# Gate and up projections of three feed-forwards: nine of eleven double turns as seven products of half sums instead of eight

## What is computed

```python
def swiglu(x, w_gu, w_down):
    g, u = jnp.split(x @ w_gu, 2, axis=-1)
    return (jax.nn.silu(g) * u) @ w_down

for l in range(2):
    x = layer_norm(ALPHA * x + 0.5 * swiglu(x, ffn1_w_gu[l], ffn1_w_down[l]), ln1_g[l], ln1_b[l])
    x = layer_norm(ALPHA * x + hybrid_mixer(x, ...), ln2_g[l], ln2_b[l])
    x = layer_norm(ALPHA * x + 0.5 * swiglu(x, ffn2_w_gu[l], ffn2_w_down[l]), ln3_g[l], ln3_b[l])
```

## Time and profile before

| | |
|---|---|
| median of 3 runs | 3521.88 us (3521.74 to 3522.15) |
| span of the profiled execution | 3520.6 us |
| TensorE busy | 3484.5 us (99%), 15956 matmuls |
| VectorE busy | 1960.7 us (56%) |
| ScalarE busy | 1381.0 us (39%) |
| GpSimd busy | 465.3 us (13%) |
| read from memory | 309.25 MB, 89 GB/s over the span |

### The profile page before, as it was taken

How to read it: one execution, slowest core, us unless ns; L and a number is a source line. 1 busy time by engine, 2 the same in 40 slices (tenths; PEclk the granted TensorE clock), 3 DMA queues, 4 the chain that set the end, 5 groups by cost and what they waited for, 6 DMA issues and landing times.

```text
span 3520.6 us, 44495 instructions
## 1 busy us (share of the span) xinstructions
PE 3484.5 (99%) x15956; PEld 2801.7 (80%) x15956; DVE 1960.7 (56%) x2532; ACT 1381.0 (39%) x1951; POOL 465.3 (13%) x321
## 2 busy tenths in 40 slices
PE   9999999999999999999999999999999999999998
PEld 6777888888777788888888876788878887678886
DVE  8888544425888644433543588533263327973324
ACT  5555433323555443323332366423243224662223
POOL 3333010001333110002100211100020003030002
PEclk9999999999999999999999999999999999999999
DMA  3112322223212222222322221222222222122222
GB/s 123 60 66 69 108 94 99 98 96 114 72 61 66 96 96 95 98 99 98 101 95 96 90 72 61 90 95 95 96 90 95 95 96 90 49 78 96 96 98 99
DMA packets 88241, 315.01 MB, mean 89 GB/s; under 512 B 10048, under 2 KB 10560, under 8 KB 87872
## 3 DMA queue, kind: packets, MB, share of 16 engines
q1 hardware_dynamic: 85824, 305.68, 25.9%
q10 hardware_dynamic: 2304, 7.80, 0.6%
HBM read 309.25 MB, written 4.19 MB: 89 GB/s over the span
## 4 chain that ended last, share of the span: by engine, by line
PE 83%; DVE 11%; DVEq 3%; ACT 2%; issue 1%; DMA 0%; SPq 0%; ACTq 0%
PE ps L1847 21%; PE ps L1848 20%; PE ps L1849 20%; PE sc L1847 5%; PE sc L1848 5%; PE sc L1849 5%; DVE w_lo L1121 3%; DVE cc_out L1703 2%; PE ps L2023 1%; DVE h_lo L1601 1%; ACT w_hi L542 1%; PE sc L2095 1%; DVEq L1459 1%; DVEq L1625 1%; PE ps L1946 0%
## 5 line engine op out<-in xcount | busy, mean ns | idle before, releaser
L1121 DVE TENSOR_TENSOR w_lo<-raw,w_hi 128x1024 fp32r<-128x1024 f32 x573 | 739.0, 1290 | 1110.4 <-ACT w_hi L542 1109.9
L542 ACT ACTIVATE w_hi<-raw 128x1024 fp32r<-128x1024 f32 x573 | 606.7, 1059 | 1412.8 <-PE ps L1849 757.2
L1847 PE MATMUL ps<-h_hi,w_hi 128*128 128x512 f32 x2576 | 1043.6, 405 | 9.3 <-DVE w_lo L1121 4.4
L1849 PE MATMUL ps<-h_hi,w_lo 128*128 128x512 f32 x2576 | 1005.4, 390 | 0.0
L1848 PE MATMUL ps<-h_lo,w_hi 128*128 128x512 f32 x2576 | 1004.4, 390 | 0.0
L1847 PEld LDWEIGHTS ps<-h_hi,w_hi 128*128 128x128 f32 x2576 | 484.5, 188 | 139.8 <-issue 40.1
L1849 PEld LDWEIGHTS ps<-h_hi,w_lo 128*128 128x128 f32 x2576 | 483.8, 188 | 103.2
L1848 PEld LDWEIGHTS ps<-h_lo,w_hi 128*128 128x128 f32 x2576 | 485.1, 188 | 92.7 <-issue 4.8
L1847 PE MATMUL ps<-hid_hi,w_hi 128*128 (+1 forms) x792 | 309.7, 391 | 0.0
L1849 PE MATMUL ps<-hid_hi,w_lo 128*128 (+1 forms) x792 | 308.2, 389 | 0.0
L1848 PE MATMUL ps<-hid_lo,w_hi 128*128 (+1 forms) x792 | 308.2, 389 | 0.0
(11 more groups left out here) (312 smaller groups left out, 4327.4 us busy)
## 6 DMA issues: line engine op xcount, KB each, us to landing
raw<-wts SPq DMA_DIRECT2D x573, 512.0 KB, 3.3
x<-xT ACTq DMA_DIRECT2D x1, 2048.0 KB, 7.9
parked<-x ACTq DMA_DIRECT2D x8, 256.0 KB, 2.0
x<-parked ACTq DMA_DIRECT2D x1, 2048.0 KB, 8.1
outT<-x SPq DMA_DIRECT2D x8, 256.0 KB, 2.1
x<-xT SPq DMA_DIRECT2D x5, 256.0 KB, 7.5
x<-xT ACTq DMA_DIRECT2D x3, 256.0 KB, 4.7
raw<-wts SPq DMA_DIRECT2D x2, 256.0 KB, 5.2
```

The source lines that it names most:

```text
L542: act(w_hi[:, s].rearrange("p a b -> p (a b)"), raw[:, s, :], ACT.Copy).then_inc(s_whi, 1)
L1121: tt(w_lo[:, s].rearrange("p a b -> p (a b)"), raw[:, s, :], w_hi[:, s].rearrange("p a b -> p (a b)").bitcast(F32), ALU.subtract).then_inc ...
L1847: mm(out, w_hi[:, s, b, :], hi, start=start, stop=False, skip_group_check=True)
L1849: return mm(out, w_lo[:, s, b, :], hi, start=False, stop=stop, skip_group_check=True)
```

## The change

The last nine double turns of gate/up in f = 3, 4 and 5 are written as a Strassen-Winograd product. The weights of one double turn (two gate tiles and two up tiles) are seen as a 2x2 matrix of blocks: A11 and A12 are the gate weights of the first and second four input tiles, A21 and A22 the up weights. The tokens are quarters: four input tiles by 256 tokens. Where eight products of a block with a quarter give gate and up, seven products of sums do:

| product | weights | tokens | bank |
|---|---|---|---|
| 0 | A11 | first inputs, first tokens | 0 |
| 1 | S2 = A11 + S1 | T2 | 1 |
| 2 | S1 = A21 + A22 | N1 | 2 |
| 3 | S3 = A11 + A21 | N3 | 1, on top |
| 4 | A12 | second inputs, first tokens | 0, on top |
| 5 | A22 | N4 | 1, on top |
| 6 | S4 = A12 + S2 | second inputs, second tokens | 2, on top |

A product is 2 x 4 x 3 = 24 matmuls of 256 columns. The token sums N1, N3, T2, N4 are made once per feed-forward, the weight sums S1 to S4 in every double turn, all by VectorE. All seven weight operands are split on the chip into high and low halves, in three slots (the third lies where `x` was). So `x` is written to memory at the end of the norm before, and read back after the last product. The host lays the four blocks of a double turn out as four chunks of the same size, so the bytes of weights stay the same.

```diff
+            def load_quads(e, c0):
+                for q in range(QUADS):
+                    a11, a12, a22, a21 = (a_wts[c0 + 4 * q + i] for i in range(4))
+                    before = PRODUCTS * (q - 1)
+                    if q:
+                        eng.wait_ge(e_lo, lo_done(e, before + 2))
+                        eng.dma_start(S1[:], a21).then_inc(e_a21, 16)
+                        eng.wait_ge(e_sum, s4_done(e, q - 1))
+                        eng.dma_start(raw[:, 0, :], a11).then_inc(s_raw[0], 16)
+                        eng.wait_ge(e_lo, lo_done(e, before + 5))
+                        eng.dma_start(A22[:], a22).then_inc(e_a22, 16)
+                        eng.wait_ge(e_lo, lo_done(e, before + 6))
+                        eng.dma_start(raw[:, 1, :], a12).then_inc(s_raw[1], 16)
...
```

TensorE, in place of the loop over double turns 2 to 10:

```diff
+                def product(b, bank, hi, lo, fresh):
+                    wh, wl = quad_w(b)
+                    eng.wait_ge(e_lo, lo_done(e, b))
+                    for t in range(2):
+                        out = bank[:, t * HALF:(t + 1) * HALF]
+                        for k in range(CHUNK // 2):
+                            i = t * (CHUNK // 2) + k
+                            mm(out, wh[:, i, :], hi[:, k, :], start=fresh and i == 0, stop=False, skip_group_check=True)
+                            mm(out, wh[:, i, :], lo[:, k, :], start=False, stop=False, skip_group_check=True)
+                            last = mm(out, wl[:, i, :], hi[:, k, :], start=False, stop=i == CHUNK - 1, skip_group_check=True)
+                    last.then_inc(e_used, 1)
...
+                    product(b, ps[0], h_hi[:, 0:4, 0:HALF], h_lo[:, 0:4, 0:HALF], True)  # waits SILU0 of the quad before
+                    product(b + 1, ps[1], T2_hi[:], T2_lo[:], True)       # waits TAKE_C21 of the quad before
+                    product(b + 2, ps[2], N1_hi, N1_lo, True)             # waits TAKE_C12; in the first quad N1's low half
+                    product(b + 3, ps[1], N3_hi[:], N3_lo[:], False)      # waits TAKE_V
...
```

VectorE. In the two plain double turns that stay it makes the token sums (with the turn's own work left as it was), then per quad:

```diff
+                    turn(0, 0, ((2, 0),), True)
+                    tt(N1[:], x[:, 0:4, 0:HALF], x[:, 0:4, HALF:], ALU.subtract).then_inc(e_sum, 1)
+                    tt(N3[:], x[:, 0:4, HALF:], x[:, 4:8, HALF:], ALU.subtract).then_inc(e_sum, 1)
+                    turn(0, 1, ((1, 1),))
+                    tt(T2[:], x[:, 4:8, HALF:], N1[:], ALU.add).then_inc(e_sum, 1)
+                    eng.drain()
+                    tt(N4[:], x[:, 4:8, 0:HALF], T2[:], ALU.subtract).then_inc(e_sum, 1)
...
+                s3(0)
+                s1(0)
+                block_lo(0, raw[:, 0, :])
+                s2(0)
+                block_lo(1, raw[:, 0, :])
+                last_plain_turn()
...
+                for q in range(QUADS):
+                    if q:
+                        c12(q - 1)
+                    block_lo(b + 2, S1[:])
+                    if q:
+                        second_product(q - 1)
+                    else:
+                        eng.wait_ge(e_hi, n1_hi_done(e))
+                        tt(N1_lo, N1[:], N1_hi.bitcast(F32), ALU.subtract).then_inc(e_lo, 1)
+                    block_lo(b + 3, S3[:])
+                    tt(up_s1, halves(ps[1]), up_s0, ALU.subtract).then_inc(e_ev, 1)      # TAKE_V
+                    block_lo(b + 4, raw[:, 1, :])
+                    tt(raw[:, 1, :], raw[:, 0, :], raw[:, 1, :], ALU.add).then_inc(e_sum, 1)      # S4
+                    if q:
+                        hidden_lo(q - 1)
+                    tt(gate_s1, halves(ps[2]), up_s0, ALU.add).then_inc(e_ev, 1)         # TAKE_W
+                    block_lo(b + 5, A22[:])
+                    tt(gate_s1, halves(ps[1]), gate_s1, ALU.subtract).then_inc(e_ev, 1)  # TAKE_C22
+                    block_lo(b + 6, raw[:, 1, :])
+                    if q < QUADS - 1:
+                        s3(q + 1)
+                        s1(q + 1)
+                        block_lo(b + 7, raw[:, 0, :])
+                        s2(q + 1)
+                    tt(up_s0, halves(ps[1]), up_s0, ALU.subtract).then_inc(e_ev, 1)      # TAKE_C21
+                    if q < QUADS - 1:
+                        block_lo(b + 8, raw[:, 0, :])
+                    tt(gate_s0, gate_s0, up_s0, ALU.mult).then_inc(e_ev, 1)              # TIMES0
+                c12(QUADS - 1)
+                split_lo(pair0 + FT, 1)
+                second_product(QUADS - 1)
+                hidden_lo(QUADS - 1)
+                eng.wait_ge(s_park, x_moved(e, 1))
```

More of the change, by code:

```diff
@@ L59 @@
 N_PLAIN = 3
+QUAD_FFNS = (3, 4, 5)
+PLAIN_TURNS = 2
+QUADS = FT // 2 - PLAIN_TURNS
+PRODUCTS = 7
+N_QUAD = 4 * QUADS
+BLOCKS = PRODUCTS * QUADS
+HALF = SEQ // 2
 N_IN2, N_OUT2 = 16, 8
@@ L478, in layer2, with quad_pairs, quad_w, hi_done @@
             return gu1, down1, w_in, w_out, gu2, gu2 + N_GU // 2
+        def quad_pairs():
+            return layer2(0)[4], layer2(1)[0], layer2(1)[4]
+        def quad_w(B):
+            slot = (0, 2, 1)[B % 3]
+            return (w_hi[:, slot], w_lo[:, slot]) if slot < 2 else (w2_hi[:], w2_lo[:])
+        def hi_done(e, b):
+            return e * (BLOCKS + 4) + b + (5 if b >= 2 else 4)
+        def lo_done(e, b):
+            return e * (BLOCKS + 4) + b + (5 if b >= 3 else 4)
+        def token_done(e, i):
+            return e * (BLOCKS + 4) + i + 1
+        def n1_hi_done(e):
+            return e * (BLOCKS + 4) + 6
+        def n1_lo_done(e):
+            return e * (BLOCKS + 4) + 7
+        def token_sums_done(e, n):
+            return e * (4 * QUADS + 4) + n
+        def s3_done(e, q):
+            return token_sums_done(e, 4) + 4 * q + 1
+        def s1_done(e, q):
+            return s3_done(e, q) + 1
+        def s2_done(e, q):
+            return s3_done(e, q) + 2
+        def s4_done(e, q):
+            return s3_done(e, q) + 3
+        def used(e, b):
+            return e * BLOCKS + b + 1
+        def act_done(e, q, step):
+            return 3 * (e * QUADS + q) + step
+        def ev_done(e, q, step):
+            return 7 * (e * QUADS + q) + step
+        def loads_done(e, q):
+            return 16 * (e * QUADS + q + 1)
+        def x_moved(e, back):
+            return 16 * (KT + 2 * e + 1 + back)
+        C1, SILU0, SILU1 = 1, 2, 3
+        TAKE_V, TAKE_W, TAKE_C22, TAKE_C21, TIMES0, TAKE_C12, TIMES1 = range(1, 8)
+        def flat(w):
+            return w.rearrange("p a b -> p (a b)")
+        def halves(bank):
+            return cube(bank[:], HALF)
         def projected(L, h, tile):
@@ L521, in _, with load_pairs @@
             eng.dma_start(par2[:], a_par2).then_inc(s_const, 16)
[L522 to L526, removed]
+            def load_pairs(lo, hi):
+                with eng.Fori(lo, hi) as pair:
+                    for s in range(2):
+                        src = a_wts[bass.ds(eng.snap(pair * 2 + s), 1)].rearrange("a p n -> p (a n)")
+                        eng.wait_ge(s_wlo, pair * 2 + s + 1)
+                        eng.dma_start(raw[:, s, :], src).then_inc(s_raw[s], 16)
@@ L527, in _ @@
+            start = 2
+            for e, gu in enumerate(quad_pairs()):
+                load_pairs(start, gu + 2 * PLAIN_TURNS)
+                load_quads(e, (gu + 2 * PLAIN_TURNS) * 2)
+                start = gu + N_GU // 2 + 1
+            load_pairs(start, DEPTH * (CH1 + CH2) // 2 + 1)
             for j, k in enumerate(DOWN_ORDER):
@@ L605, in gate_up @@
                 eng.preload_act_table_set("silu_and_others")
-                if scaled:
-                    turn(0, ())
-                else:
-                    turn(0, ((2, 0),), ((1, 1),), folded)
-                with eng.Fori(1, FT // 2) as j:
-                    turn(j)
-                eng.preload_act_table_set("natural_log_exp_and_others")
+                if f in QUAD_FFNS:
+                    turn(0, ((2, 0),), ((1, 1),), folded)
+                    quad_turns(QUAD_FFNS.index(f), pair0, f)
+                else:
+                    if scaled:
+                        turn(0, ())
+                    else:
+                        turn(0, ((2, 0),), ((1, 1),), folded)
+                    with eng.Fori(1, FT // 2) as j:
+                        turn(j)
@@ L853, in _, with layer_norm @@
             eng.dma_start(sin2[:], a_c2[:, 3 * P + SEQ:3 * P + 2 * SEQ]).then_inc(s_const2, 16)
-            def layer_norm(i, L, c0, order):
+            def layer_norm(i, L, c0, order, park=False):
                 n = 3 * L + i
@@ L1910, in gate_up @@
                     turn(0, 1)
-                with eng.Fori(1, FT // 2) as j:
-                    turn(j, 0)
-                    turn(j, 1)
+                if f in QUAD_FFNS:
+                    turn(1, 0)
+                    turn(1, 1)
+                    seven(QUAD_FFNS.index(f), f)
+                else:
+                    with eng.Fori(1, FT // 2) as j:
+                        turn(j, 0)
+                        turn(j, 1)
             def down(pair0, f, centre=None):
@@ L1923, in turn @@
```

(11 more changed lines are left out.)

234 lines of the change are left out of this document (220 added, 14 removed).

## The result

The changed kernel takes 3490.12 us (median of 4, 3489.85 to 3491.25), the kernel before, beside it, 3521.81: 31.7 us less, ratio 0.9911 (0.9897 to 0.9924). The forecast was 3486.

A forecast was written before the change was run, and what follows sets the result against it. TensorE's own rate was taken to bound the kernel. The terms -43.2, +6 (way in) and +1.5 (way out) gave -35.7 us, from 3521.88 to 3486.2 us; 3462 to 3508 was to hold 8 in 10.

The forecast's parts named there:

- TensorE's sum: TensorE in the 27 double turns: 168 matmuls of 0.120 us, 20.16 us instead of 21.76, together -43.2 us.
- Rival 1: In the turns: 256-column matmuls take 0.1133 us or less and VectorE's 19.5 us decide; 3468 us, chance 0.3.
- Rival 2: In the turns: TensorE's matmul period is longer than 0.120 us; at 0.125, 3509 us; chance 0.08.
- Rival 4: In the turns: weight loads are not hidden, 168 x 0.22 = 37 us, +410, 3930 us; chance 0.04.
- VectorE's loop: VectorE's queue in one turn, waits included, takes 19.1 to 19.6 us, under TensorE's 20.16, so it stays hidden.
- My sign: In a turn of seven products, VectorE would show about 19.5 us busy.
- Rival 3: In the turns: VectorE's operations start 0.09 us after the one before ends; 22.4 us a turn, 3546 us; chance 0.08.
- The way in: Start of the seven products, three times: TensorE stands about 2.0 us for N1's low half, +6 us.
- No stands inside the turns: TensorE is busy all through each turn; the tightest hand-over, S2's low half, is ready 1.2 us early.
- my own signs: The forecast is wrong if TensorE waits inside the turns, or if the matmul spacing is over 0.125 us.
- The way out: After the last product, three times: VectorE stands until x is back from memory, 0.5 us taken, +1.5 us.
- the forecast case: Whole kernel: 0.120 us a matmul, VectorE hidden; 3486.2 us, own range 3476 to 3500, chance 0.5.

The follow-up runs named there:

- the halves: The kernel before with every 512-column matmul of 30 gate/up double turns written as two of 256 columns, no products of sums: 3560.02 us (ratio 1.0108).

## Why the prediction was right, step by step

- TensorE's sum, -43.2: measured -44.6. The matmul of 256 columns is 0.1197 us on average (20.11/168) against 0.120. The choice between 0.1133 and 0.120 was the one open point of size; the starts of the changed kernel decided it, and the halves showed that it is the form's own. Rivals 1, 2 and 4 fell with it.
- VectorE's loop, 19.1 to 19.6 under 20.16: held. TensorE is busy all of 20.10 us in an undisturbed turn. The kernel with 2.6 us more VectorE work, at 21.74 us a turn, agrees with the size of the loop, and shows that busy time alone would have misled; the one with 1.3 us more was worse than the loop gives. My sign, VectorE "about 19.5 us busy" in a turn, was wrong: it is busy 18.1 to 18.5, as the sum without its waits (17.9) says; I had named the loop with its waits as busy time. Rival 3 fell: its 22.4 us a turn are not there, and followers start early, as in the earlier trace rows.
- The way in, 3 x 2.0 = +6: measured +9.0, the term sized worst but for the one that I had at nothing (next). The wait was the one named. VectorE's timeline at f = 3 has N1's low half behind S1's:

```profile
2264.92 1.23 DVE L1470 TENSOR_TENSOR w_lo<-S,w_hi 128x1024 fp32r<-128x1024 f32 x1 [1.51 <-ACT w_hi L786]
2266.07 1.22 DVE L1524 TENSOR_TENSOR h_lo<-N,h_hi 128x1024 fp32r<-128x1024 f32 x1
```

  N1's low half ended 8.0 us after TensorE had begun the seven products (2267.29 against 2259.31) in f = 3 and 8.4 in f = 5, not 7.7, so TensorE's starts were 2.4 to 2.8 us apart there, 7.5 us in all three. The clock's fall, which I did not have at all, added the other 1.5 in f = 4.
- No stands inside the turns: wrong by 3.6 us, and TensorE waiting inside the turns was one of my own signs that the forecast is wrong. It came true in six of 27 turns; the sum survived because the stands are short. I had S2's low half ready 1.2 us ahead and A22's landing at 3.3 us, its median, and did not ask how late it can be. Nor was the lead 1.2 us. The five late loads had S1 start 0.9, 1.1, 1.5, 1.5 and 2.4 us later than the usual 3.3 us after issue, and the turns behind them lost 0.2, 0.4, 0.7, 0.7 and 1.6: each time 0.8 us were covered.
- The way out, 3 x 0.5: measured 0.3 in f = 4 and nothing in f = 3 and 5. Within its bounds of nothing to 1 us.

The sum was -35.7, the result -31.7. That it is off by only 4 is in part luck. What I had for the first turns was 3.0 us too small and for the longer ones 3.6, together 6.6; against that TensorE's beat gained 1.4 us more than I had, and the ways out cost 1.2 less. The two terms missed are the clock and the late landings, and what they cost can be had back almost whole by order alone: 3477.5. The range of the forecast case, 3476 to 3500, is also a little narrower than its own bounds add up to (3471 to 3501, with the way out at 1.5).

## What the runs showed that I had not expected

Late landings go together with instruction fetches. The code of the 27 turns is written out, and the instruction queue has 109 packets of 16 KB instead of 73. In the changed kernel five of A22's loads had S1 start 4.2 to 5.7 us after their issue, instead of 3.1 to 3.4 as in the other turns from the third on; all five had such a packet start 1.1 to 2.6 us into the load, and none of the others had one before 2.9 us. The six longer turns are those behind these five loads (the latest reaches into two). In the other six kernels with all 27 turns of this kind the same five loads landed 4.2 to 5.7 us after issue, each with such a packet 1.0 to 3.0 us in. Some others were late without one in the two kernels with more VectorE work (up to 4.3 us). Queues of the changed kernel (kind, packets, MB, share; then count, KB, us to landing) around the latest, then around one without a fetch:

```profile
q8 instruction: 1, 0.02, 1.3%
...
A<-wts SPq DMA_DIRECT2D x1, 512.0 KB, 5.7
```

```profile
q1 hardware_dynamic: 177, 0.62, 57.1%
...
A<-wts SPq DMA_DIRECT2D x1, 512.0 KB, 3.3
```

And VectorE in the two turns:

```profile
2779.26 1.22 DVE L1482 TENSOR_TENSOR S<-S,A 128x1024 f32<-128x1024 f32 x1 [2.85 <-DMA A<-wts]
```

```profile
2756.77 1.23 DVE L1482 TENSOR_TENSOR S<-S,A 128x1024 f32<-128x1024 f32 x1 [0.47 <-DMA A<-wts]
```

That the fetch delays the load is read from these coincidences and not shown: A22's load for the second turn of f = 3 landed after 4.4 us with no such packet beside it, while the engines moved other loads, and a kernel with the turns in a loop, which would have less code to fetch, was not tried. That the late landing made the longer turns is shown by the new order of S1: there the five loads landed as late as ever (4.4 to 5.3 us), and all turns behind the first but one were at 20.11.

The clock fell in some first turns and not in others with the same stand: over the five kernels that kept the wait for N1, in 9 of 14 first turns, with 2.4 to 2.8 us between the starts on both sides of the stand, at a price of some 1.5 us each. The length of the stand does not tell them apart: 2.46 us came with the fall and without. In the kernels without the stand it fell in none of nine.

## What to carry to other kernels

When fewer columns are bought with more matmuls, price the matmul, not the columns: here each cost its columns plus 0.0133 us at the upper clock, and in a row of short ones the weight load, 0.111 us, set the distance instead. When the next engine comes close to the bound (here VectorE was busy in nine tenths of the turn), add up its queue in order, with its waits for its own results and for transfers, at their late end and not their median. And look at the first turn and the last by themselves: a fifth of this gain went there, 9.3 of 44.6 us, and nearly all of it came back by doing first what TensorE wants first.
